# Rounded weight halves numbered over the split units only, and a tail with both residual tiles in natural order

## What is computed

```python
g_sel = argmax(xf @ w_group + b_group);  two experts of 8 inside that group
y = (silu(x @ w1[e]) * (x @ w3[e])) @ w2[e]          # 32 experts, 2048 -> 512 -> 2048
h = layer_norm(ALPHA * h + sum_k e_w[k] * y[k], ln2_g, ln2_b)
```

## Time and profile before

| | |
|---|---|
| median of 3 runs | 2134.13 us (2132.72 to 2134.97) |
| the profiled execution: its own time | 2134.49 us |
| its span, first to last instruction | 2132.7 us |
| TensorE busy | 2049.1 us, 96% of the span |
| VectorE busy | 1555.0 us, 73% |
| ScalarE busy | 1192.5 us, 56% |
| GpSimd busy | 135.7 us, 6% |
| DMA | 613.47 MB, mean 288 GB/s |

### The profile page before, as it was taken

How to read it: one execution, slowest core, us unless ns; L and a number is a source line. 1 busy time by engine, 2 the same in 40 slices (tenths; PEclk the granted TensorE clock), 3 DMA queues, 4 the chain that set the end, 5 groups by cost and what they waited for, 6 DMA issues and landing times.

```text
span 2132.7 us, 27841 instructions
## 1 busy us (share of the span) xinstructions
PE 2049.1 (96%) x10774; PEld 1669.2 (78%) x10774; DVE 1555.0 (73%) x1498; ACT 1192.5 (56%) x967; POOL 135.7 (6%) x92
## 2 busy tenths in 40 slices
PE   8999999999999999999999999999999999999996
PEld 8998888899999998887887767667777666766663
DVE  7656664453646375454769999999999999999987
ACT  5445653333333323334346777777777777777773
POOL 1000000000000000001000111011110111011010
PEclk9999999999999999999999999999999999999998
DMA  6554335655454544667779999999999999999993
GB/s 215 158 140 158 118 119 185 209 181 170 147 177 146 169 157 155 220 216 256 227 286 366 410 426 427 426 427 427 424 426 426 420 422 422 417 415 421 410 426 159
DMA packets 143693, 613.47 MB, mean 288 GB/s; under 512 B 19057, under 2 KB 31489, under 8 KB 116257
## 3 DMA queue, kind: packets, MB, share of 16 engines
q1 hardware_dynamic: 137760, 601.14, 73.2%
q0 software_dynamic: 5856, 11.26, 1.5%
HBM read 612.87 MB, written 24.13 MB: 299 GB/s over the span
## 4 chain that ended last, share of the span: by engine, by line
PE 64%; DMA 12%; DVE 11%; issue 8%; ACT 3%; POOL 1%; POOLq 0%; DVEq 0%; ACTq 0%
PE ps L2023 18%; PE ps L2004 15%; DMA raw<-in_w_dram 7%; DVE wl L801 6%; PE ps L1152 5%; PE ps L1153 5%; DMA xrows<-xscr,rowno 4%; PE ps L2381 4%; PE ps L1149 4%; ACT wh L641 2%; DVE yall L973 2%; PE ps L2136 2%; PE ps L1174 1%; PE ps L2096 1%; PE ps L2109 1%
## 5 line engine op out<-in xcount | busy, mean ns | idle before, releaser
L801 DVE TENSOR_TENSOR wl<-raw,wh 128x2048 fp32r<-128x2048 f32 x320 | 720.4, 2286 | 72.0 <-ACT wh L641 71.0
L641 ACT ACTIVATE wh<-raw 128x2048 fp32r<-128x2048 f32 x320 | 604.4, 1912 | 184.6 <-PE ps L1153 82.0
L1578 DVE TENSOR_TENSOR wl<-raw,wh 128x2048 fp32r<-128x2048 f32 (+1 forms) x168 | 379.7, 2263 | 286.5 <-ACT wh L1382 286.4
L1382 ACT ACTIVATE wh<-raw 128x2048 fp32r<-128x2048 f32 (+1 forms) x168 | 317.9, 1894 | 447.4 <-DMA raw<-in_w_in_dram 276.4
L1152 PE MATMUL ps<-wh,xg 128*128 128x512 f32 x776 | 329.8, 425 | 33.7 <-DVE wl L801 33.4
L1153 PE MATMUL ps<-wl,xg 128*128 128x512 f32 x776 | 303.7, 391 | 0.0
L2004 PE MATMUL ps<-hth,wh 128*128 128x272 f32 (+1 forms) x896 | 259.7, 290 | 3.2 <-DVE wl L1578 1.8
L2004 PE MATMUL ps<-htl,wh 128*128 128x272 f32 (+1 forms) x896 | 255.8, 285 | 0.0
L2004 PE MATMUL ps<-hth,wl 128*128 128x272 f32 (+1 forms) x896 | 255.5, 285 | 0.0
L1149 PE MATMUL ps<-raw,xg 128*128 128x512 f32 x496 | 222.9, 592 | 0.0
L1152 PEld LDWEIGHTS ps<-wh,xg 128*128 128x128 f32 x776 | 145.9, 188 | 86.0 <-DVE wl L801 38.3
(11 more groups left out here) (369 smaller groups left out, 2918.0 us busy)
## 6 DMA issues: line engine op xcount, KB each, us to landing
raw<-in_w_dram SPq DMA_DIRECT2D x192, 2048.0 KB, 16.9
raw<-in_w_in_dram SPq DMA_DIRECT2D x103, 1024.0 KB, 5.1
raw<-in_w_pa_dram SPq DMA_DIRECT2D x16, 1024.0 KB, 5.0
raw<-in_w_pb_dram SPq DMA_DIRECT2D x16, 1024.0 KB, 5.1
raw<-in_w_out_dram SPq DMA_DIRECT2D x16, 1024.0 KB, 5.1
raw<-in_w_ukv_dram SPq DMA_DIRECT2D x8, 1024.0 KB, 5.4
yscr<-zeros SPq DMA_DIRECT2D x4, 1024.0 KB, 8.4
yrow<-yscr SPq DMA_DIRECT2D x4, 1024.0 KB, 19.6
```

What stands on the lines that cost most here:

```text
L641: nc.scalar.activation(wh2[:, x % HELD, :], raw_of(turn, x), ACT.Copy).then_inc(s_wh2, 1)
L801: nc.vector.tensor_tensor(wl_of(turn, x), raw_of(turn, x), wh2[:, x % HELD, :].bitcast(F32), ALU.subtract).then_inc(s_wl2, 1)
L1382: nc.scalar.activation(wh[:, n % RING1, 0:c], raw1[:, n % RING1, 0:c], ACT.Copy).then_inc(s_wh, 1)
L1578: nc.vector.tensor_tensor(wl[:, n % RING1, 0:c], raw1[:, n % RING1, 0:c], wh[:, n % RING1, 0:c].bitcast(F32), ALU.subtract).then_inc(s_wl, 1)
```

## The change

**Numbering.** `SPLITS` lists the 20 split units; `shifted(x, by)` gives the unit that is `by` split units further; `held(x)` is place `X_SPLIT[x % 24] % HELD`. So `hi(x)` now waits for the split unit four split units back, and step x, where x itself is split, holds `hi` and `lo` of the split unit four further on; a step whose x is whole holds none. Step 0 of the first pair, which held none, now holds unit 5; step 1 unit 6, step 2 unit 7, step 3 unit 8, step 4 none.

**Tail.** ScalarE makes `xn0`, a copy of `xb0` in natural order, at k = 23 of the last pair, and TensorE reads `xn0` in `stream_back(0)`. `last_pair_back(0)` starts its first two chunks when the first half of `last_rest` is done (`s_half_out`). For tile 1 TensorE alternates `stream_back` and `last_pair_back` chunk by chunk. The add of tile 1 (`choices(1)`) moves from VectorE to GpSimd, behind `s_all`, the two row loads and the add of tile 0; VectorE waits for it only before it collects tile 1.

```diff
@@ -288,6 +288,7 @@
         X_SPLIT = [sum(y not in XR for y in range(x)) for x in range(25)]
+        SPLITS = [x for x in range(24) if x not in XR]
         PAIRS = N_EXP // 2
...
@@ -317,6 +318,7 @@
         xb0 = place("xb0", [P, KD, P], 139264)
+        xn0 = place("xn0", [P, D_MODEL], 65536)
         xrows = place("xrows", [P, KD, P], 98304)
...
@@ -405,6 +407,7 @@
         s_yh = sem("s_yh")
+        s_half_out = sem("s_half_out")
         s_ye = [sem(f"s_ye{i}") for i in range(2)]
...
@@ -412,7 +415,7 @@
         s_stc = sem("s_stc")
-        s_own = sem("s_own")
+        s_own = [sem(f"s_own{i}") for i in range(TT)]
         s_cmb = sem("s_cmb")
...
@@ -432,6 +435,14 @@
             return (24 - len(XR)) * (turn + x // 24) + X_SPLIT[x % 24]
+
+        def shifted(x, by):
+
+            n = len(SPLITS) * (x // 24) + X_SPLIT[x % 24] + by
+            return 24 * (n // len(SPLITS)) + SPLITS[n % len(SPLITS)]
+
+        def held(x):
+            return wh2[:, X_SPLIT[x % 24] % HELD, :]
 
...
@@ -618,6 +629,10 @@
                 nc.gpsimd.tensor_tensor(marks[:, 5:6], half[:, 0:1], half[:, 0:1], ALU.mult).then_inc(s_all, 1)
+                for r in range(2):
+                    pool.wait_ge(s_y[2 + r], 16 * rounds)
+                pool.wait_ge(s_yy, TT * rounds - 1)
+                nc.gpsimd.tensor_tensor(acc[:, 1, :], acc[:, 1, :], yrow[:, 1, 1, :], ALU.add).then_inc(s_yy, 1)
 
...
@@ -631,14 +646,12 @@
             def hi(turn, x):
-                if whole(turn, x):
-                    return
                 landed2(act, turn, x)
-                if isinstance(turn, int) and 24 * turn + x <= HELD:
+                if isinstance(turn, int) and split_units(turn, x) < HELD:
                     act.wait_ge(s_wused, N_UNITS)
                 else:
-                    done(act, turn, x - HELD)
-                nc.scalar.activation(wh2[:, x % HELD, :], raw_of(turn, x), ACT.Copy).then_inc(s_wh2, 1)
+                    done(act, turn, shifted(x, -HELD))
+                nc.scalar.activation(held(x), raw_of(turn, x), ACT.Copy).then_inc(s_wh2, 1)
 
...
@@ -691,8 +704,8 @@
                         copy_up(turn, x, 2 * turn + 1, 1)
-                    if x + HELD != HELD or not early:
-                        hi(turn, x + HELD)
+                    if not whole(turn, x) and not (last and x == 19):
+                        hi(turn, shifted(x, HELD))
                     if k == 14 and early:
...
@@ -709,6 +722,10 @@
                         outputs(turn, x, 2 * turn, 0, turn)
+                    if k == 23 and last:
+                        act.wait_ge(s_back, 16 * rounds)
+                        nc.scalar.activation(xn0[:, :].rearrange("q (p k) -> q k p", k=KD), xb0[:, :, :],
+                                             ACT.Copy).then_inc(s_own[0], 1)
                     if k == 20 and last:
...
@@ -716,7 +733,7 @@
                         nc.scalar.activation(xn1[:, :].rearrange("q (p k) -> q k p", k=KD), xs[:, 1, :, :],
-                                             ACT.Copy).then_inc(s_own, 1)
+                                             ACT.Copy).then_inc(s_own[1], 1)
                     for q in range(GQ):
...
@@ -795,10 +812,8 @@
             def lo(turn, x):
-                if whole(turn, x):
-                    return
                 dve.wait_ge(s_wh2, split_units(turn, x) + 1)
-                nc.vector.tensor_tensor(wl_of(turn, x), raw_of(turn, x), wh2[:, x % HELD, :].bitcast(F32),
+                nc.vector.tensor_tensor(wl_of(turn, x), raw_of(turn, x), held(x).bitcast(F32),
                                         ALU.subtract).then_inc(s_wl2, 1)
...
@@ -949,11 +964,11 @@
 
-            def choices(t, rounds):
+            def choices(rounds):
 
                 for r in range(2):
-                    dve.wait_ge(s_y[2 * t + r], 16 * rounds)
-                nc.vector.tensor_tensor(acc[:, t, :], acc[:, t, :], yrow[:, t, 1, :], ALU.add).then_inc(s_yy, 1)
+                    dve.wait_ge(s_y[r], 16 * rounds)
+                nc.vector.tensor_tensor(acc[:, 0, :], acc[:, 0, :], yrow[:, 0, 1, :], ALU.add).then_inc(s_yy, 1)
 
...
@@ -963,7 +978,7 @@
                     m = nc.vector.scalar_tensor_tensor(y, ps[r, b:b + 2, :], wsc[r, 1:2], y, ALU.mult, ALU.add)
-                m.then_inc(s_ye[1], 1)
+                    m.then_inc((s_half_out, s_ye[1])[c], 1)
 
...
@@ -989,7 +1004,8 @@
                         hidden(2 * turn, 0, turn)
-                    lo(turn, x + HELD)
+                    if not whole(turn, x) and not (last and x == 19):
+                        lo(turn, shifted(x, HELD))
                     if k in (3, 10) and early:
...
@@ -1022,9 +1038,8 @@
                 pair(turn + PAIRS - 1, PAIRS - 1, 1, last=True)
-                choices(0, rounds)
+                choices(rounds)
                 last_rest(turn + PAIRS - 1, rounds)
-                choices(1, rounds)
                 return more if early else None
...
@@ -1049,13 +1064,14 @@
 
-            dve.wait_ge(s_yy, TT * (more + 1))
+            dve.wait_ge(s_yy, TT * more + 1)
             for c in range(3):
...
             dve.wait_ge(s_acc, 1)
+            dve.wait_ge(s_yy, TT * (more + 1))
             for c in range(4):
...
@@ -1149,7 +1165,7 @@
                     else:
-                        nc.tensor.matmul(o, s, wh2[:, x % HELD, c:c + 512], start=st, stop=False, skip_group_check=True)
+                        nc.tensor.matmul(o, s, held(x)[:, c:c + 512], start=st, stop=False, skip_group_check=True)
                         m = nc.tensor.matmul(o, s, wl_of(turn, x)[:, c:c + 512], start=False, stop=sp_,
...
@@ -1242,19 +1258,16 @@
 
-            def stream_back(t):
-
-                for c in range(4):
-                    nc.tensor.matmul(ps[:, FINAL_BANK[t][c], :], ident[:, :],
-                                     xn1[:, 512 * c:512 * (c + 1)] if t else
-                                     xb0[:, :, 32 * c:32 * (c + 1)].rearrange("q k p -> q p k"),
-                                     start=True, stop=False, skip_group_check=True)
-
-            def last_pair_back(t):
-
-                for c in range(4):
-                    nc.tensor.matmul(ps[:, FINAL_BANK[t][c], :], selt[:, P * t:P * (t + 1)], yall[:, 512 * c:512 * (c + 1)],
-                                     start=False, stop=True, skip_group_check=True).then_inc(s_cmb, 1)
+            def stream_back(t, c):
+
+                own_tile = (xn0, xn1)[t]
+                nc.tensor.matmul(ps[:, FINAL_BANK[t][c], :], ident[:, :], own_tile[:, 512 * c:512 * (c + 1)],
+                                 start=True, stop=False, skip_group_check=True)
+
+            def last_pair_back(t, c):
+
+                nc.tensor.matmul(ps[:, FINAL_BANK[t][c], :], selt[:, P * t:P * (t + 1)], yall[:, 512 * c:512 * (c + 1)],
+                                 start=False, stop=True, skip_group_check=True).then_inc(s_cmb, 1)
 
...
@@ -1273,13 +1286,19 @@
                 pe.wait_ge(s_ye[0], last + 1)
-                pe.wait_ge(s_back, 16 * rounds)
-                stream_back(0)
+                pe.wait_ge(s_own[0], rounds)
+                for c in range(4):
+                    stream_back(0, c)
+                pe.wait_ge(s_half_out, rounds)
+                for c in range(2):
+                    last_pair_back(0, c)
                 pe.wait_ge(s_ye[1], last + 1)
-                last_pair_back(0)
-                pe.wait_ge(s_own, rounds)
-                stream_back(1)
-                last_pair_back(1)
+                for c in range(2, 4):
+                    last_pair_back(0, c)
+                pe.wait_ge(s_own[1], rounds)
+                for c in range(4):
+                    stream_back(1, c)
+                    last_pair_back(1, c)
 
...
```

## The result

The changed kernel takes 2146.80 us (median of 4 runs, 2144.15 to 2149.81), the kernel before 2133.49 (median of 4, 2132.72 to 2134.97): ratio 1.0062, 95% interval 1.0048 to 1.0077. It is slower by 13.3 us, where 1.2 us less was forecast, and lies outside the range. The profiled execution has its own time of 2146.93 us and a span of 2145.1.

What follows compares the result with a forecast made beforehand. It took DMA weight loads to bound the experts' stage, and engine order the first pair, last pair and tail. First pair +2.6, last pair +1.1, tail -4.9 gave -1.2 us: 2134.13 to 2132.9 us, range 2129.8 to 2136.2.

Steps and rivals of the forecast that it cites:

- The tail: After the last unit: tile 1's collects and statistics lie beside TensorE, statistics ending at 2112.98 instead of 2117.87; -4.9 us.
- The first turn: First pair: one more lo early delays VectorE's steps and TensorE's freeing of places; +2.6 us on all landings, bounds 0 and 3.1.
- the walk: First pair, step by step: number_rows at 1135.5, mix near 1153.5, unit 12 near 1159.6, third gather 2.6 us late.
- its terms for `hidden`: First pair: hidden stands behind lo(13), 2.23 + 0.41 + 0.35 - 0.47, given as about 2.6 us late.
- its own bounds: Whole kernel: limits of the forecast's own terms, given as 2131.9 to 2134.0 us for the forecast case, chance 0.50.
- The steady part: Experts' stage bound by DMA: holding a rounded copy one unit longer only brings TensorE nearer the landings; worth 0.
- the numbering pays in the steady part: Rival, steady part: TensorE's 3.8% idle closes if TensorE bounded; with DMA at 1.01 it gives 0; no separate chance.
- The last turn: Last pair: hi(19) ahead of copy_up makes the second mix start at 2082.07, +1.1 us, bounds 0 and 1.5.
- a repeated delay in the second turn: Rival, second pair: hidden and gathered_rest again behind one more lo, another 2.6 us or somewhat more, 2136.0; chance 0.16.

Runs made afterwards that it cites:

- e1: Kernel before with the new tail alone; numbering, waits and steps of hi and lo as before: 2129.03 us, ratio 0.9976.
- e8: Changed kernel with the old order of hi and lo in the first turn, the extra unit of lead taken at that turn's end: 2139.07 us, ratio 1.0026.
- e3: Changed kernel with the fetch of the next turn's rows issued ahead of the first scatter instead of behind it: 2135.21 us, ratio 1.0008.
- e4: Changed kernel with twelve small products, result never read, ahead of TensorE's wait for the fetched rows: 2139.41 us, ratio 1.0036.
- e2: Kernel before with the new numbering alone, keeping the old tail: 2152.85 us, ratio 1.0087.
- e7: Changed kernel with unit 19's rounded copy moved behind copy_up again in the last turn: 2144.27 us, ratio 1.0048.
- e9: Changed kernel with rows' fetch first, lead taken at the first turn's end, and copy_up ahead of unit 19's rounded copy in the last: 2128.22 us, ratio 0.9971.
- e6: Changed kernel with the new places and waits, but each hi and lo at its old step: 2128.50 us, ratio 0.9972.

## Why the prediction was wrong

**The tail: right.** -4.9 forecast, -4.5 in e1, and each row where it was put: 29.5 us from `stream_back(0)` to the end, the add on GpSimd hidden (4.56 us, between the bounds of 2.29 and 7.5).

**The first turn: right in its steps, wrong in its size.** `number_rows` at 1135.29 (1135.5 forecast), the first `mix` at 1153.69 (1153.5). There the walk ends: it took TensorE to work at full clock behind its wait of 1.73 us, and it worked at 0.51 from 1155 to 1162. Unit 12 began at 1161.10, not 1159.6, though `hidden` was done by 1159.80: TensorE was still at unit 11. And the third `gather` at 1168.68, 4.4 us late and not 2.6. On the landings that is +6.7 for +2.6. e8 takes it away. Two small slips in the working matter little: its terms for `hidden` add up to 2.5, not 2.6, and its own bounds give 2129.2 to 2133.8, not 2131.9 to 2134.0.

```profile
1159.38 0.42 DVE L964 TENSOR_TENSOR hx<-hv,hx 128x256 fp32r<-128x256 f32 x1
...
1161.10 0.63 PE L1168 MATMUL ps<-wh,hx 128*128 128x512 f32 x1
...
1168.68 0.52 PE L1135 MATMUL ps<-ident,xrows 128*128 128x128 f32 x3 [0.62 <-DVE xg L810]
```

**The steady part: the step that failed.** "Where DMA bounds, a rounded copy held one unit longer only brings TensorE nearer to the landings. ... Worth 0." TensorE was busy 461.65 of 480 us there, under 4% from being the bound, and I priced its waits as slack without asking for what it would wait next. It ran into the next thing that was late, the fetched rows, for which it already waited 13 times, by up to 1.4 us. That row of the waits was in the trace of before. What I took as a rival in the other direction (the numbering pays in the steady part) should have had its mirror: a lead on one input lengthens the wait on another. The lag grows from 6.7 us at the 13th load to 13.5 at the 181st, where the kernel before has 0. e3 removes the growth by the rows alone, so the wait for them is where it starts. e4 removes most of it by the clock alone, so the wait costs mainly by the slow stretch behind it.

**The last turn: the wait right, the clock left out.** `copy_up` behind `hi(19)` held up `mix` by 1.54 us (1.1 forecast), and 7 us at a clock of 0.51 came behind. From the 181st landing to the start of `stream_back(0)` lie 72.2 us, before 68.3: +3.9 for +1.1. The wait alone, in e3 and e4, makes it 68.9, +0.6; the slow stretch, for which the prediction had no term, is the other 3.3.

The sum with measured terms, on the spans: first turn +6.7, steady part +6.8, last turn +3.9, tail -4.9, together +12.5; the spans differ by 2145.1 - 2132.7 = 12.4. The terms are those of this one pair of traces; in e2 and e7 the steady part took 11.2 and 12.3.

The rival on the slower side, a repeated delay in the second turn, was the wrong mechanism: the growth is small in each turn and has nothing to do with VectorE's order.

This case's traces fit the Trainium skill, "TensorE: Matmul & The Clock Gate", section "HAM oscillation — how this bites in real kernels": there a wait that returns with each tile throttles TensorE again each time, so that every tile starts at the half clock. Here it returned with each turn: in the second, 3.73 us of wait and then a clock of 0.50.

## What to carry to other kernels

An engine that is 96% busy in a stage bound by DMA is not slack but a second bound close behind. Before an edit brings it forward, look in the view of waits for every other thing that it waits for, even briefly, and see how far each is from being late; and count, behind a TensorE wait that the edit makes or lengthens, the chance of some us at half clock (it came in the changed kernel behind waits of 1.54 to 3.73 us, and in others not behind each such wait). Where each engine's order is written out by hand, the steps by which work is put ahead matter more than the buffers that permit it: take the lead where the engine has time (at the end of the first turn, not at its start), and keep copies that another engine waits for ahead of ones that wait for a landing.

## What the runs showed of the hardware

The clock doesn't fall after every wait of such a length. It fell behind 1.73 us in the first turn and 1.54 us in the last of the changed kernel; in the kernel before TensorE waited as long, and the clock stayed at 1.00:

```profile
2026.61 0.47 PE L1152 MATMUL ps<-wh,xg 128*128 128x512 f32 x1 [1.54 <-DVE wl L801]
```

In e3 and e4 it stayed up even behind the same wait, at the same place, 1.52 and 1.54 us ahead of the last `mix`. What tells these cases apart the runs don't show. Nor does a low clock by itself tell of a loss: e9 at 0.97 and e6 at 0.99 take the same time.
